# First tile of the input projection by row blocks of the weights, and output projection one product at a time

## The chip, the cores and the metric

The kernel runs on one core of one Trainium2 chip. The metric is the time of one execution on the device in microseconds; of several runs the median is compared. TensorE (PE) does matrix products and transposes into the eight banks of PSUM, the vector engine (DVE) and the scalar engine (ACT) do elementwise work, GpSimd (POOL) small elementwise work, and SyncE (SP) issues nearly all DMAs. Each engine runs its own instruction stream in order; they meet at semaphores.

## The reference

One layer of a hybrid decoder: 2048 tokens, width 1024, float32.

```
hn  = rmsnorm(x, g_mix_pre);  z = hn @ w_in            # 1024 -> 1604 columns
q, k, v, q_idx, k_idx, w_idx, zp = split(z)            # 8 query heads, 2 kv heads, 4 indexer heads
score[t,s] = sum_h w_idx[t,h] * relu(q_idx[t,h] . k_idx[s])    # causal
sel  = top-k keys of score per query, k = 256
attn = softmax over sel of (q . k) @ v                 # rotary on 16 dims of each head
pool = trailing means 2/4/8/16 of zp minus zp, a 128x128 map for each group, a scale
h  = x + rmsnorm(concat(attn, pool) @ w_o, g_mix_post)
h += rmsnorm(relu(rmsnorm(h, g_mlp_pre) @ w_up)^2 @ w_down, g_mlp_post)
h += rmsnorm(sigmoid(h @ w_ple_gate) * (p @ w_ple_proj), g_ple_post)
```

## The kernel before, in words

Tokens are cut into T = 16 tiles of 128, widths into K = 8 row blocks of 128. Where float32 accuracy matters an operand is split into a high part (type fp32r) and a low part, and a product is done as three matmuls, hi·hi, hi·lo and lo·hi (`split_product`).

**Stage 1, the input projection.** SP issues the small loads (pos_i, g_pre_col, pool_scale_col, g_mlp_col, w_pool_sb, all counted by `small_ld`), then x of tiles 0 and 1, then w_in in eight row blocks of 128 x 1604 (`w_in_raw`), counted by two semaphores of four blocks each. ACT makes `w_in_hi` (L930) with the gain g_pre, DVE `w_in_lo` (L1326). Ahead of that DVE computes the angles of the rotary tables (L1126 to L1140, each operation waiting for the one before) and ACT their sine (L854). For each tile ACT squares x (`square_x`), DVE and POOL make 1/rms and scale (`norm`), TensorE transposes x into banks 0 and 1 (`transpose_x`), ACT and DVE take it out in two halves as `hnT_hi` and `hnT_lo` (`evacuate_hnT`). TensorE then makes z of the tile in four column groups, `project_to` for banks 2 (0 to 512), 3 (to 1024), 4 (68 columns) and 5 (the pooling columns), each over k = 0 to 7. Between the groups of tile i stand `transpose_pool(i - 1)`, `transpose_k(i - 1)` and `transpose_x(i + 1)`. `rope` on DVE rotates q and k with the tables. The search for the top-k thresholds of tiles 2 to 7 runs on ACT and DVE beside the projection.

**Stage 2, the attention.** All (head, key block) pairs of all tiles are one list of steps m; a tile i has 8 heads of 1, 2, 3 or 4 key blocks (tiles 0 to 3, 4 to 7, 8 to 11, 12 to 15). At step m TensorE computes score blocks about two heads ahead (`score_block`, L1601 and L1602), transposes the probabilities of step m + 2 (`turn_probs`, L1687), multiplies those of step m with the values (`weigh`, L1701) and does index products of the search (`search_part`). DVE adds the mask and takes the maximum (`mask_block`, L1368), ACT does exp and copies the transposed probabilities to SBUF (`probsT`, L1015). The search of tiles 8 to 15 is spread over the steps up to head 5 of tile 13: each round has one count on DVE (L1230) and one on ACT (L912), and the threshold moves when both are done. Tile i - 1's output projection (16 products 128x128 by 128x512, L1721) is done in the heads of tile i: behind head 1 `transpose_o`; behind the last step of heads 2, 3 four products each into bank 0 for the left half of the columns (n = 0), behind heads 4, 5 for n = 1. ACT moves mixT out of PSUM at head 2 and the two results (`evacuate_mix`, L977 and L980) at heads 4 and 6.

```
if last_of(H, b) and i >= 1:
    if h == 1:
        transpose_o(i - 1)
    if h in (2, 3):
        output_projection(i - 1, 0, range(4 * (h - 2), 4 * (h - 1)))
    if h in (4, 5):
        output_projection(i - 1, 1, range(4 * (h - 4), 4 * (h - 3)))
```

**Stage 3, the MLP and the per-layer embedding**, in four chunks of 512 tokens, begins when stage 2 is over.

Of the kernel before, what the change touches and what calls it, by code (L numbers as in the profile page):

```python
# [47 lines left out]
def hybrid_block(nc, x, p, positions, g_mix_pre, w_in, w_pool, pool_scale, w_o, g_mix_post,  # L48
# [30 lines left out]
    with ExitStack() as ctx:  # L79
# [3 lines left out]
        def sem(name):  # L83
            return ctx.enter_context(nc.semaphore(name))
# [137 lines left out]
        w_in_ld = [sem("w_in_ld_low"), sem("w_in_ld_high")]  # L222
# [198 lines left out]

        AHEAD_BLOCKS = 2
# [100 lines left out]
        def over(cols, width):  # L523

            return cols.unsqueeze(2).to_broadcast([P, cols.shape[1], width])
# [10 lines left out]
        def _(sp):  # L536
            def row_over_partitions(dst, src):
                return sp.dma_start(dst, src.to_broadcast([P, D]))

            sp.dma_start(pos_i[:], positions[0].rearrange("(t p) -> p t", p=P),  # L540
                         allow_slow_non_contiguous=True).then_inc(small_ld, 16)
            for dst, src in ((g_pre_col, g_mix_pre), (pool_scale_col, pool_scale), (g_mlp_col, g_mlp_pre)):
# [4 lines left out]
            def load_x(i, u):  # L547
                sp.dma_start(x_in[:, u, :], x_tiles[i]).then_inc(x_ld[u], 16)

# [302 lines left out]
        def _(act):  # L852
            act.wait_ge(turns_rdy, 1)
            nc.scalar.activation(trig[:], turns[:], ACT.Sin).then_inc(trig_rdy, 1)  # L854

# [67 lines left out]
            act.wait_ge(setup_step, 4 + ROT_HALF + G)  # L923
            act.wait_ge(small_ld, 16 * 5)
            junk_early = kept_early[:, 512:1024].bitcast(BF16)
            square_x(0)
            square_x(1)
            for k in range(K):
                act.wait_ge(w_in_ld[k // (K // 2)], 16 * K // 2)
                nc.scalar.activation(w_in_hi[:, k, :], w_in_raw[:, k, :], ACT.Identity,  # L930
                                     scale=g_pre_col[:, k:k + 1]).then_inc(w_in_hi_rdy, 1)
# [3 lines left out]

            evacuate_hnT(0, 0)
            for i in range(T):
                evacuate_hnT(i, 1)
                if i >= 1:
                    copy_pool_rows(i - 1)  # L940
                if i + 2 < T:
                    square_x(i + 2)
                if i >= 1:
                    search_part(4 * i - 1, junk_early)
                evacuate_za(i, i % 2)
                if i >= 1:
                    evacuate_pool(i - 1)
                search_part(4 * i, junk_early)
                evacuate_zb(i, i % 2)
                if i >= 1:  # L950
                    evacuate_k(i - 1)
# [163 lines left out]
        def _(dve):  # L1115
            dve.wait_ge(small_ld, 16 * 5)
            dve.wait_ge(setup_step, 4 + ROT_HALF + G)
            done = [0]

            def link(ins):  # L1120
                done[0] += 1
                ins.then_inc(rot_setup, 1)
                dve.wait_ge(rot_setup, done[0])


            link(nc.vector.tensor_copy(pos_f[:], pos_i[:]))  # L1126
            link(nc.vector.tensor_tensor(angle[:], over(pos_f[:], ROT_HALF),
                                         freq[:].unsqueeze(1).to_broadcast([P, T, ROT_HALF]), ALU.mult))
            for n, (quarter, shift) in enumerate(((0.0, 0.0), (0.25, float(np.pi / 2)))):
                link(nc.vector.tensor_scalar(turns[:, n], angle[:], float(1 / (2 * np.pi)), quarter, ALU.mult, ALU.add))  # L1130
                link(nc.vector.tensor_scalar(turns[:, n], turns[:, n], ROUND, None, ALU.add))
                link(nc.vector.tensor_scalar(turns[:, n], turns[:, n], -ROUND, None, ALU.add))
                rest = angle[:]
                for part in TWO_PI:
                    link(nc.vector.scalar_tensor_tensor(out=trig[:, n], in0=turns[:, n], scalar=float(-part), in1=rest,
                                                        op0=ALU.mult, op1=ALU.add))
                    rest = trig[:, n]
                link(nc.vector.tensor_scalar(turns[:, n], trig[:, n], shift, None, ALU.add))
                link(nc.vector.tensor_scalar(turns[:, n], turns[:, n], PI_SAFE, -PI_SAFE, ALU.min, ALU.max))
            nc.vector.tensor_copy(rot[:, 0, 0:1, 0:1], turns[:, 0, 0:1, 0:1]).then_inc(turns_rdy, 1)  # L1140

# [23 lines left out]
            def rope(i, u):  # L1165
                dve.wait_ge(za_ev, i + 1)
# [153 lines left out]

            norm(0, 0)

            for k in range(K):

                dve.wait_ge(w_in_hi_rdy, k + 1)
                nc.vector.scalar_tensor_tensor(out=w_in_lo[:, k, :], in0=w_in_raw[:, k, :], scalar=g_pre_col[:, k:k + 1],  # L1326
                                               in1=w_in_hi[:, k, :].bitcast(F32), op0=ALU.mult,
                                               op1=ALU.subtract).then_inc(w_in_lo_rdy, 1)
            norm(1, 1)
            dve.wait_ge(trig_rdy, 1)  # L1330
            evacuate_hnT(0, 0)
            for i in range(T):
                evacuate_hnT(i, 1)
                if i >= 1:
                    rope(i - 1, (i - 1) % 2)
                    early_part(4 * i - 1)
# [5 lines left out]
                if i >= 1:  # L1342
                    evacuate_k(i - 1)
# [197 lines left out]
        def _(pe):  # L1541
            pe.wait_ge(const_rdy, sum(WINDOWS) - G + 2)
            pe.wait_ge(small_ld, 16 * 5)
# [25 lines left out]
            def pool_product(i):  # L1569
                pe.wait_ge(mixer_step, 10 * i + 9)  # L1570
# [11 lines left out]
            def project_to(b, lo, hi, done_sem, first=False, fresh=None, half_sem=None):  # L1582
                for k in range(K):
                    if fresh is not None and k % 4 == 0:
                        pe.wait_ge(hnT_lo_rdy, 2 * fresh + k // 4 + 1)
                    if first:
                        pe.wait_ge(w_in_lo_rdy, k + 1)
# [43 lines left out]

            transpose_x(0)
            for i in range(T):
                pe.wait_ge(za_ev, i)
                project_to(2, 0, Z_A, za_ps, i == 0, fresh=i)
                if i >= 2:
                    pool_product(i - 2)
                if i >= 1:
                    transpose_pool(i - 1)
# [3 lines left out]
                if i >= 1:  # L1643
                    transpose_k(i - 1, (i - 1) % 2)
# [100 lines left out]
            for m, (H, b) in enumerate(steps):  # L1745
# [131 lines left out]
```

## Time and profile before

| what | value |
|---|---|
| median of 3 runs | 3360.23 us (3358.62 to 3362.65) |
| the profiled execution | 3354.67 us |
| its span | 3353.1 us |
| its mean granted TensorE clock | 0.947 |
| TensorE, DVE, ACT, POOL busy | 3053.1, 1684.7, 1334.7, 336.3 us |
| stage 1, 2, 3 (from, to) | 0 to about 430, to about 1543, to 3353 us |

The profile is of one execution. A row of its timeline gives the start, the length and the engine of an instruction or of several merged ones; what stands in brackets is the idle time before it and what ended it. The clock column is the TensorE clock that was granted, as a share of 2.4 GHz. Matmul ends are modelled, so rows overlap a little. A few matmul records are missing.

### The profile page before, as it was taken

What the parts mean: (1) busy time and instruction counts of PE and PEld (TensorE: products, weight loads), DVE (VectorE), ACT (ScalarE), POOL (GpSimd) and SP (SyncE); (2) the same over time, 40 slices, a digit from 0 to 9 for tenths busy, and PEclk for the clock granted to TensorE, in tenths of its full rate; (3) what the DMA queues carried; (4) which work ended last, traced back from release to release, by engine and by line L of the source; (5) the groups of instructions that cost most, each with busy time, mean ns of one, the idle gap of its engine ahead of it and who ended that gap; (6) DMA issues with size and microseconds to landing.
All of it is one profiled execution on the core that took longest, in us unless ns stands there. A gap on an engine that the chain in (4) does not pass through costs nothing.

```text
span 3353.1 us, 38038 instructions
## 1 busy us (share of the span) xinstructions
PE 3053.1 (91%) x13944; PEld 2353.3 (70%) x13944; DVE 1684.7 (50%) x3373; ACT 1334.7 (40%) x2162; POOL 336.3 (10%) x431
## 2 busy tenths in 40 slices
PE   5999968788888888996999989999999999999998
PEld 4877856565666776884788847888568886588873
DVE  3376777777866777631333343333433333433333
ACT  3253455756656477553322223222232222222221
POOL 1332322121120310000000000000000000000000
PEclk9999989798887878998999999999999999999999
DMA  3111142111201110105423303233123322133210
GB/s 118 60 53 57 36 124 58 53 52 35 62 20 30 45 35 22 54 23 186 136 90 101 120 31 119 88 101 120 48 79 113 101 89 94 58 119 101 88 50 26
DMA packets 215456, 250.92 MB, mean 75 GB/s; under 512 B 57952, under 2 KB 160096, under 8 KB 215264
## 3 DMA queue, kind: packets, MB, share of 16 engines
q1 hardware_dynamic: 212960, 239.99, 22.5%
q10 hardware_dynamic: 2304, 8.39, 0.6%
q8 instruction: 118, 1.93, 0.2%
q14 instruction: 74, 0.61, 0.1%
HBM read 208.34 MB, written 40.01 MB: 74 GB/s over the span
## 4 chain that ended last, share of the span: by engine, by line
issue 59%; PE 26%; DVE 7%; ACT 4%; POOL 2%; DMA 1%; SPq 0%; DVEq 0%; POOLq 0%; ACTq 0%
PE bank L1579 7%; PE bank L1721 6%; PE bank L1701 5%; PE bank L1601 2%; PE bank L1687 2%; PE bank L1602 2%; ACT kept L912 2%; DVE kept L1230 1%; DVE probs L1368 1%; ACT probsT L1015 1%; ACT score_tail L912 1%; DVE too_few L1238 1%; POOL rstdC L847 1%; POOL score L823 1%; PE bank L1550 1%
## 5 line engine op out<-in xcount | busy, mean ns | idle before, releaser
L1443 DVE TENSOR_TENSOR w_lo<-w_raw,w_hi 128x1024 fp32r<-128x1024 f32 x256 | 312.6, 1222 | 520.5 <-ACT w_hi L1058 514.8
L1058 ACT CAST w_hi<-w_raw 128x1024 fp32r<-128x1024 f32 x256 | 267.4, 1045 | 562.0 <-PE bank L1579 535.0
L1701 PE MATMUL bank<-values,probsT 128*128 128x64 f32 x2176 | 334.7, 301 | 149.7 <-ACT probsT L1015 124.6
L1701 PEld LDWEIGHTS bank<-values,probsT 128*128 128x128 f32 x2176 | 313.7, 219 | 176.7 <-ACT probsT L1015 162.8
L1579 PE MATMUL bank<-hn_hi,w_hi 128*128 128x512 f32 x1024 | 400.3, 391 | 14.9 <-DVE hn_lo L1460 10.7
L1579 PE MATMUL bank<-w_hi,hid_lo 128*128 128x512 f32 x1024 | 405.9, 396 | 0.0
L1579 PE MATMUL bank<-w_lo,hid_hi 128*128 128x512 f32 x1024 | 405.9, 396 | 0.0
L1579 PE MATMUL bank<-w_hi,hid_hi 128*128 128x512 f32 x1024 | 405.9, 396 | 0.0
L1579 PE MATMUL bank<-hn_lo,w_hi 128*128 128x512 f32 x1024 | 399.7, 390 | 0.0
L1579 PE MATMUL bank<-hn_hi,w_lo 128*128 128x512 f32 x1024 | 399.4, 390 | 0.0
L1368 DVE CUSTOM_DVE_ANT_0 probs<-bank,mask 128x384 f32<-128x384 f32 (+3 forms) x320 | 193.7, 607 | 234.4 <-PE bank L1602 232.3
L912 ACT ACTIVATE kept<-score,threshold 128x1024 bf16<-128x1024 f32 (+4 forms) x160 | 251.9, 1574 | 112.2 <-DVE threshold L1247 91.8
L1230 DVE TENSOR_SCALAR_CACHE_REDUCE kept<-score,threshold 128x896 bf16<-128x896 f32 (+4 forms) x160 | 267.7, 1673 | 0.7
L1721 PE MATMUL bank<-wo_sb,mixT_t 128*128 128x512 f32 x512 | 247.0, 628 | 2.2 <-ACT h_t L980 1.1
L1478 DVE CAST hid_hi<-square 128x512 fp32r<-128x512 f32 x128 | 54.7, 427 | 366.0 <-ACT square L1083 366.0
L1081 ACT ACTIVATE square<-bank 128x512 f32<-128x512 f32 x128 | 76.6, 599 | 403.7 <-PE bank L1579 403.7
L1579 PEld LDWEIGHTS bank<-hn_hi,w_hi 128*128 128x128 f32 x1024 | 192.9, 188 | 56.9 <-issue 16.4
L1849 PE MATMUL bank<-w_gate_sb,h3T 128*128 128x512 f32 x512 | 227.1, 602 | 0.0
L1579 PEld LDWEIGHTS bank<-w_hi,hid_lo 128*128 128x128 f32 x1024 | 192.8, 188 | 47.0
L1579 PEld LDWEIGHTS bank<-w_hi,hid_hi 128*128 128x128 f32 x1024 | 192.9, 188 | 46.9
L1579 PEld LDWEIGHTS bank<-w_lo,hid_hi 128*128 128x128 f32 x1024 | 192.9, 188 | 46.9
L1579 PEld LDWEIGHTS bank<-hn_hi,w_lo 128*128 128x128 f32 x1024 | 192.9, 188 | 40.3
(191 smaller groups left out, 4754.4 us busy)
## 6 DMA issues: line engine op xcount, KB each, us to landing
w_raw<-in_w_up SPq DMA_DIRECT2D x64, 1024.0 KB, 5.6
w_raw<-in_w_down SPq DMA_DIRECT2D x64, 1024.0 KB, 5.0
x_in<-in_x SPq DMA_DIRECT2D x16, 512.0 KB, 3.7
q_t<-q_scratch SPq DMA_DIRECT2D x32, 256.0 KB, 3.7
x_t<-in_x SPq DMA_DIRECT2D x16, 512.0 KB, 4.3
h_scratch<-h_t SPq DMA_DIRECT2D x16, 512.0 KB, 2.9
hnT_scratch<-hn2T_t SPq DMA_DIRECT2D x16, 512.0 KB, 3.9
hn_lo<-hnT_scratch SPq DMA_DIRECT2D x4, 2048.0 KB, 11.3
```

The lines of the kernel that those rows point to most:

```text
L912: nc.scalar.activation(junk[:, 0:P * (t + 2)], score_of(t + 1), ACT.Sign, scale=-1.0, bias=threshold[:, 1:2].bitcast(F32), accum_out=below ...
L1058: nc.scalar.copy(w_hi[:, p % 4, :].rearrange("p (k f) -> p k f", f=piece_width(p)), raw_piece(p)).then_inc(w_hi_rdy, 1)
L1081: nc.scalar.activation(square[:, f % 2, :], bank[:, UP[q % 2][f % 2], :], ACT.Relu).then_inc(relu2_step, 1)
L1230: nc.vector.tensor_scalar(junk[:, 0:P * (t + 1)], score_of(t), threshold[:, 0:1].bitcast(F32), -float(P), ALU.is_lt, ALU.add, accum_out=be ...
L1368: nc.vector.tensor_tensor_reduce(out=probs[:, H % 3, o:o + w], in0=bank[:, ring_bank[("s", H, b)], 0:w], in1=mask[:, i % 2, o:o + w], scal ...
L1443: nc.vector.tensor_tensor(out_p, raw_piece(p), hi_p.bitcast(F32), ALU.subtract).then_inc(w_lo_rdy, 1)
L1579: ins = nc.tensor.matmul(dst, lhs[a], rhs[b], start=(first and n == 0), stop=(last and n == 2))
L1601: nc.tensor.matmul(dst, hi, k_parts[:, key, o:o + w], start=True, stop=False)
L1602: return nc.tensor.matmul(dst, lo, k_parts[:, key, o:o + w], start=False, stop=True)
L1701: last = nc.tensor.matmul(bank[:, 4, h * HEAD:(h + 1) * HEAD], probsT[:, m % 3, a * P:(a + 1) * P], values[:, kt, HEAD * kv:HEAD * (kv + 1 ...
L1721: last = nc.tensor.matmul(bank[:, mix_bank(i, n), :], mixT_t[:, k, :], wo_sb[:, k, n * 512:(n + 1) * 512], start=(k == 0), stop=(k == K - 1))
L1849: last = nc.tensor.matmul(bank[:, (2, 4)[n], :], h3T[:, a % 2, k, :], w_gate_sb[:, k, n * 512:(n + 1) * 512], start=(k == 0), stop=(k == K ...
```

## The change

The loads: x of tile 0 is issued first, then g_pre_col with a semaphore of its own, w_in row blocks 0 to 3, x of tile 1, blocks 4 to 7, and then the other small loads. Each row block has a semaphore. The first tile has a function of its own on TensorE, `project_first_tile`: k is the outer loop, and each k is multiplied into all four banks; `transpose_x(1)` stands after k = 5. ACT and DVE split the row blocks in three groups (0, 1 to 3, 4 to 7) with the hnT halves of tiles 0 and 1 and the squares and norms between them. The rotary tables are made behind the last hnT half of tile 1; ACT waits for them ahead of `copy_pool_rows(0)`, and `rope` waits for the sine. The loops over tiles start at 1.

In the attention the products of the output projection are laid out by a table `mix_at`: for each half n the eight k are spread over the steps of two heads after the first of them, and stand ahead of `weigh(m)`.

```diff
+        mix_at = {}
+        for i in range(1, T):
+            for n in range(2):
+                first = Q_HEADS * i + 2 + 2 * n
+                places = range(head_first[first] + 1, head_first[first + 2])
+                for k in range(K):
+                    mix_at.setdefault(places[k * len(places) // K], []).append((i - 1, n, k))
...
+            load_x(0, 0)
+            sp.dma_start(g_pre_col[:], g_mix_pre[0].rearrange("(k p) -> p k", p=P),
+                         allow_slow_non_contiguous=True).then_inc(g_pre_ld, 16)
+            load_w_in(range(0, K // 2))
+            load_x(1, 1)
+            load_w_in(range(K // 2, K))
             sp.dma_start(pos_i[:], positions[0].rearrange("(t p) -> p t", p=P),
...
-            load_x(0, 0)
-            load_x(1, 1)
-            for k in range(K):
-                sp.dma_start(w_in_raw[:, k, :], w_in[0, k * P:(k + 1) * P, :]).then_inc(w_in_ld[k // (K // 2)], 16)
...
+            square_x(0)
+            act.wait_ge(g_pre_ld, 16)
+            split_weights(range(0, 1))
             evacuate_hnT(0, 0)
+            evacuate_hnT(0, 1)
+            split_weights(range(1, 4))
+            square_x(1)
+            split_weights(range(4, K))
+            evacuate_hnT(1, 0)
+            evacuate_za(0, 0)
+            evacuate_hnT(1, 1)
+            evacuate_zb(0, 0)
+            evacuate_zc(0, 0)
+            act.wait_ge(setup_step, 4 + ROT_HALF + G)
+            act.wait_ge(small_ld, 16 * 4)
+            act.wait_ge(turns_rdy, 1)
+            nc.scalar.activation(trig[:], turns[:], ACT.Sin).then_inc(trig_rdy, 1)
+            copy_pool_rows(0)
+            square_x(2)
...
             norm(0, 0)
+            dve.wait_ge(g_pre_ld, 16)
+            split_weights(range(0, 1))
+            evacuate_hnT(0, 0)
+            evacuate_hnT(0, 1)
+            split_weights(range(1, 4))
+            norm(1, 1)
+            split_weights(range(4, K))
+            evacuate_hnT(1, 0)
+            evacuate_hnT(1, 1)
+            rotations()
+            norm(2, 0)
...
+            def project_first_tile():
+
+                for k in range(K):
+                    if k % 4 == 0:
+                        pe.wait_ge(hnT_lo_rdy, k // 4 + 1)
+                    pe.wait_ge(w_in_lo_rdy, k + 1)
+                    for b, lo, hi, done_sem in ((2, 0, Z_A, za_ps), (3, Z_A, Z_B, zb_ps), (4, Z_B, Z_POOL, zc_ps), (5, Z_POOL, W_IN, zp_ps)):
+                        last = split_product(bank[:, b, 0:hi - lo], (hnT_hi[:, k, :], hnT_lo[:, k, :]),
+                                             (w_in_hi[:, k, lo:hi], w_in_lo[:, k, lo:hi]), k == 0, k == K - 1)
+                        if k == K - 1:
+                            last.then_inc(done_sem, 1)
+                    if k == 3:
+                        last.then_inc(half_used, 1)
+                    if k == 5:
+                        transpose_x(1)
...
+                for i_mix, n, k in mix_at.get(m, ()):
+                    output_projection(i_mix, n, range(k, k + 1))
                 weigh(m)
...
-                    if h in (2, 3):
-                        output_projection(i - 1, 0, range(4 * (h - 2), 4 * (h - 1)))
-                    if h in (4, 5):
-                        output_projection(i - 1, 1, range(4 * (h - 4), 4 * (h - 3)))
```

## Rows read from the trace of the kernel before

**Rows 1.** The page: busy us, share of the span, instructions.

```profile
PE 3053.1 (91%) x13944; PEld 2353.3 (70%) x13944; DVE 1684.7 (50%) x3373; ACT 1334.7 (40%) x2162; POOL 336.3 (10%) x431
```

**Rows 2.** Timeline of the start: start us, us, engine line op out<-in.

```profile
0.73 0.43 SPq L540 DMA_DIRECT2D pos_i<-in_positions  x1
...
6.96 0.17 DVE L1126 CAST pos_f<-pos_i 128x16 f32<-128x16 int32 x1 [6.96 <-DMA w_pool_sb<-in_w_pool]
...
12.57 1.04 ACT L900 ACTIVATE score_tail<-x_in 128x1024 bf16<-128x1024 f32 x1
...
15.54 1.94 PE L1550 MATMUL bank<-ident,x_in 128*128 128x128 f32 x8 [15.54 <-DVE x_in L1146]
...
18.12 6.20 ACT L930 ACTIVATE w_in_hi<-w_in_raw,g_pre_col 128x1604 fp32r<-128x1604 f32 x4 [3.19 <-DMA w_in_raw<-in_w_in]
...
27.94 7.29 DVE L1326 SCALAR_TENSOR_TENSOR w_in_lo<-w_in_raw,g_pre_col,w_in_hi 128x1604 fp32r<-128x1604 f32 x4 [0.86 <-ACT w_in_hi L930]
...
36.63 1.28 DVE L1151 TENSOR_TENSOR hnT_lo<-bank,hnT_hi 128x512 fp32r<-128x512 f32 x2
...
37.41 0.77 PE L1579 MATMUL bank<-w_in_hi,hnT_hi 128*128 128x512 f32 x1 [19.93 <-DVE hnT_lo L1151]
```

**Rows 3.** Tile w_in_raw and tile x_in: loads of each, and time to landing.

```profile
L557 SPq DMA_DIRECT2D w_in_raw<-in_w_in x8: 432/448/652, 5.4 to 9.2; - x8
...
DMA to landing us min/median/max: 6.8/12.1/17.0
...
DMA to landing us min/median/max: 3.4/4.7/10.0
```

**Rows 4.** The timeline of the scalar engine at the first change of tile.

```profile
60.38 0.59 ACT L885 CAST hnT_hi<-bank 128x512 fp32r<-128x512 f32 x1 [2.17 <-PE bank L1579]
...
65.86 0.60 ACT L860 ACTIVATE zs<-bank 128x512 f32<-128x512 f32 x1 [3.36 <-PE bank L1579]
```

**Rows 5.** The timeline of the scalar engine at its first table load.

```profile
0.74 1.28 ACT L854 ACT_TABLE_LOAD   x1 [0.74 <-PEq L1866]
```

**Rows 6.** The waits of 586 to 1360 us: total us, times, longest.

```profile
DVE probs L1368 <- PE bank L1602: 130.2, 65, 6.9
...
PE bank L1701 <- ACT probsT L1015: 107.8, 69, 4.6
```

**Rows 7.** The timeline of TensorE and of the vector engine around one projection run.

```profile
976.43 6.17 PE L1721 MATMUL bank<-wo_sb,mixT_t 128*128 128x512 f32 x8
...
983.10 0.69 DVE L1368 CUSTOM_DVE_ANT_0 probs<-bank,mask 128x512 f32<-128x512 f32 x1 [6.00 <-PE bank L1602]
```

**Rows 8.** Windows: length, busy PE, PEld, DVE, ACT, POOL, clock, DMA.

```profile
964.00:967.00 3.00, 3.00 (x7) 1.30 (x7) 0.22 (x2) 1.00 (x2) 0.00 (x0) 0.93 0.00 0
...
973.00:976.00 3.00, 1.70 (x10) 1.46 (x9) 2.93 (x8) 2.54 (x4) 0.00 (x0) 0.78 0.00 0
...
976.00:979.00 3.00, 3.00 (x6) 1.55 (x7) 1.10 (x2) 2.68 (x5) 0.00 (x0) 0.50 0.00 0
```

**Rows 9.** Windows over heads 2 to 5 of eight of the tiles.

```profile
549.00:580.00 31.00, 29.54 (x137) 19.18 (x135) 20.72 (x37) 10.38 (x22) 12.72 (x14) 1.00 0.20 51
...
608.00:641.00 33.00, 28.35 (x119) 18.56 (x118) 19.51 (x62) 20.60 (x41) 0.00 (x0) 0.87 0.08 17
...
664.00:697.00 33.00, 28.48 (x134) 19.28 (x134) 23.61 (x73) 24.20 (x43) 0.00 (x0) 0.95 0.07 17
...
794.00:835.00 41.00, 33.99 (x156) 23.55 (x157) 25.71 (x70) 27.24 (x43) 0.00 (x0) 0.88 0.06 14
...
943.00:994.00 51.00, 43.58 (x199) 30.40 (x197) 30.86 (x76) 28.16 (x42) 7.92 (x8) 0.87 0.05 11
...
1035.00:1089.00 54.00, 45.16 (x204) 31.79 (x203) 33.12 (x84) 35.28 (x51) 0.00 (x0) 0.83 0.05 10
...
1230.00:1289.00 59.00, 49.29 (x232) 37.47 (x232) 39.59 (x95) 40.64 (x56) 0.00 (x0) 0.82 0.04 9
...
1404.00:1446.00 42.00, 42.00 (x261) 32.75 (x260) 12.61 (x38) 19.07 (x32) 0.00 (x0) 1.00 0.00 1
```

More of the change, by code:

```diff
@@ L219, in hybrid_block @@
         mlp_stack.close()
-        w_in_ld = [sem("w_in_ld_low"), sem("w_in_ld_high")]
+        g_pre_ld = sem("g_pre_ld")
+        w_in_ld = [sem(f"w_in_ld_{k}") for k in range(K)]
         w_in_hi_rdy = sem("w_in_hi_rdy")
@@ L921, in search_part, with split_weights @@
                     count_below(t, k, junk)
-            act.wait_ge(setup_step, 4 + ROT_HALF + G)
-            act.wait_ge(small_ld, 16 * 5)
-            junk_early = kept_early[:, 512:1024].bitcast(BF16)
[L926 to L931, printed above, removed]
+            def split_weights(ks):
+                for k in ks:
+                    act.wait_ge(w_in_ld[k], 16)
+                    nc.scalar.activation(w_in_hi[:, k, :], w_in_raw[:, k, :], ACT.Identity,
+                                         scale=g_pre_col[:, k:k + 1]).then_inc(w_in_hi_rdy, 1)
+            junk_early = kept_early[:, 512:1024].bitcast(BF16)
             def copy_pool_rows(i):
@@ L934, in copy_pool_rows @@
                 nc.scalar.copy(zp_rows[:], bank[:, 5, :]).then_inc(zp_rows_ev, 1)
+            square_x(0)
+            act.wait_ge(g_pre_ld, 16)
+            split_weights(range(0, 1))
             evacuate_hnT(0, 0)
-            for i in range(T):
-                evacuate_hnT(i, 1)
-                if i >= 1:
+            evacuate_hnT(0, 1)
[13 more added lines that the diff above has]
+            square_x(2)
+            for i in range(1, T):
+                if i >= 2:
+                    evacuate_hnT(i, 1)
                     copy_pool_rows(i - 1)
@@ L1115, in _ @@
         def _(dve):
[L1116 to L1140, printed above, removed]
             def norm(i, u):
@@ L1165, in rope @@
             def rope(i, u):
+                dve.wait_ge(trig_rdy, 1)
                 dve.wait_ge(za_ev, i + 1)
@@ L1319, in early_part @@
                 weigh_early(at["index"].get(spot, ()))
-            norm(0, 0)
[L1323 to L1328, printed above, removed]
-            norm(1, 1)
-            dve.wait_ge(trig_rdy, 1)
@@ L1331, in _, with rotations, link @@
[L1331 to L1336, printed above, removed]
+            def rotations():
+                dve.wait_ge(small_ld, 16 * 4)
+                dve.wait_ge(setup_step, 4 + ROT_HALF + G)
+                done = [0]
+                def link(ins):
+                    done[0] += 1
+                    ins.then_inc(rot_setup, 1)
+                    dve.wait_ge(rot_setup, done[0])
+                link(nc.vector.tensor_copy(pos_f[:], pos_i[:]))
+                link(nc.vector.tensor_tensor(angle[:], over(pos_f[:], ROT_HALF),
+                                             freq[:].unsqueeze(1).to_broadcast([P, T, ROT_HALF]), ALU.mult))
+                for n, (quarter, shift) in enumerate(((0.0, 0.0), (0.25, float(np.pi / 2)))):
+                    link(nc.vector.tensor_scalar(turns[:, n], angle[:], float(1 / (2 * np.pi)), quarter, ALU.mult, ALU.add))
+                    link(nc.vector.tensor_scalar(turns[:, n], turns[:, n], ROUND, None, ALU.add))
+                    link(nc.vector.tensor_scalar(turns[:, n], turns[:, n], -ROUND, None, ALU.add))
+                    rest = angle[:]
+                    for part in TWO_PI:
+                        link(nc.vector.scalar_tensor_tensor(out=trig[:, n], in0=turns[:, n], scalar=float(-part), in1=rest,
+                                                            op0=ALU.mult, op1=ALU.add))
+                        rest = trig[:, n]
+                    link(nc.vector.tensor_scalar(turns[:, n], trig[:, n], shift, None, ALU.add))
+                    link(nc.vector.tensor_scalar(turns[:, n], turns[:, n], PI_SAFE, -PI_SAFE, ALU.min, ALU.max))
+                nc.vector.tensor_copy(rot[:, 0, 0:1, 0:1], turns[:, 0, 0:1, 0:1]).then_inc(turns_rdy, 1)
@@ new lines, in split_weights @@
+            def split_weights(ks):
+                for k in ks:
+                    dve.wait_ge(w_in_hi_rdy, k + 1)
+                    nc.vector.scalar_tensor_tensor(out=w_in_lo[:, k, :], in0=w_in_raw[:, k, :], scalar=g_pre_col[:, k:k + 1],
+                                                   in1=w_in_hi[:, k, :].bitcast(F32), op0=ALU.mult,
+                                                   op1=ALU.subtract).then_inc(w_in_lo_rdy, 1)
+            norm(0, 0)
+            dve.wait_ge(g_pre_ld, 16)
@@ new lines, in _ @@
+            split_weights(range(0, 1))
+            evacuate_hnT(0, 0)
+            evacuate_hnT(0, 1)
+            split_weights(range(1, 4))
+            norm(1, 1)
+            split_weights(range(4, K))
[3 more added lines that the diff above has]
+            norm(2, 0)
+            for i in range(1, T):
+                if i >= 2:
+                    evacuate_hnT(i, 1)
+                rope(i - 1, (i - 1) % 2)
+                early_part(4 * i - 1)
@@ L1630, in search_part @@
                 index(at["index"].get(spot, ()))
+            def project_first_tile():
[12 more added lines that the diff above has]
+                        transpose_x(1)
             transpose_x(0)
-            for i in range(T):
+            project_first_tile()
+            for i in range(1, T):
                 pe.wait_ge(za_ev, i)
-                project_to(2, 0, Z_A, za_ps, i == 0, fresh=i)
+                project_to(2, 0, Z_A, za_ps, fresh=i)
                 if i >= 2:
                     pool_product(i - 2)
-                if i >= 1:
-                    transpose_pool(i - 1)
+                transpose_pool(i - 1)
                 search_part(4 * i)
@@ L1642, in _ @@
                 project_to(3, Z_A, Z_B, zb_ps)
-                if i >= 1:
-                    transpose_k(i - 1, (i - 1) % 2)
+                transpose_k(i - 1, (i - 1) % 2)
                 search_part(4 * i + 1)
```

34 lines of the change are left out of this document (15 added, 19 removed).

## The prediction

> **What bounds the kernel now.** I read the page first. TensorE is busy 91% of the span, so the question is where the other 9% lies and at which clock the 91% is spent [rows 1]. The 40 slices show three stages: the projection of x to about 430 us, the attention with its top-k search to about 1543 us, the MLP from there. The change touches the start of the first and heads 2 to 5 of each tile of the second. The MLP has no edited line and no start time of its own, so it moves as a block.
>
> *The start.* The timeline shows the vector engine making the rotation tables first, from 6.96 us; the sine must be done before the scalar engine squares x (12.57), so tile 0 is transposed only at 15.54 [rows 2]. The weights land one row block per 2.0 us: eight loads issued from 5.4 to 9.2 us take 6.8 us (the first) to 17.0 us (the last), so blocks 0 to 7 arrive at 12.2, 14.2 ... 26.2 [rows 3]. Two semaphores, each for four blocks, let the split into high and low parts begin only at 18.12 and 26.27; the last low part ends at 27.94 + 7.29 = 35.2, and TensorE's first projection matmul starts at 37.41 [rows 2]. From there TensorE sets the pace: tile 0 ends at 60.4, where the scalar engine can take the next hnT half, and the first column group of tile 1 at 65.9 [rows 4].
>
> *The attention.* By the waits of 586 to 1360 us TensorE waits 107.8 us in L1701 for the scalar engine's copy of probsT, and the vector engine waits 130.2 us for score blocks [rows 6]. Both hang together around the output projection. One product of it is two recorded passes; a run of four lasts about 3.65 us at full clock, longer at half. In the timeline the run that begins at 976.43 keeps the score matmuls away until 982; the vector engine idles 6.00 us up to 983.10, so the counting of the search stops too [rows 7]. In the steps ahead of such a run it is TensorE that idles: 1.70 us busy of 3 just before the run, after which the granted clock is 0.50, that is 1.2 GHz instead of 2.4, and it is at this clock that the run starts [rows 8].
>
> **Part 1, the first tile.** Removed from the path: the rotation chain, the sine and four small loads ahead of x; the two four-block waits; and the order by column group (bank 2, then 3, 4, 5). Nothing is added: 96 projection matmuls as before, k outermost. Worked forward:
> - x is issued at 0.73. A load of its size took 3.4 us alone [rows 3], so it lands at 4.2. From the square over the norm to the first transpose takes 15.5 − 12.6 = 3.0 us, the transposes 1.94 [rows 2]: done at 9.1.
> - g_pre_col and block 0 are issued behind x. x and block 0 together are 1.3 MB; I put block 0 at 6.9, the next at 2.0 us each, and x of tile 1 (1.3 us) in fourth place: 8.9, 10.9, 12.9, then 16.1 to 22.1.
> - High parts cost 1.55 us each, low parts 7.29/4 = 1.82, an hnT half 0.65 [rows 2]. Low part 0 ends at 10.4, the two hnT halves at 11.1 and 11.7. The first projection matmul starts at **11.1**. Low parts 1 to 3 end at 13.6 to 17.2, the norm of tile 1 at 18.8, low parts 4 to 7 at 20.6 to 26.1.
> - TensorE needs 60.38 − 37.41 = 22.97 us for the tile, cold start and the transposes of tile 1 included [rows 2, 4], about 2.4 us per k at full clock (a 512-wide column group takes 5.5 us for its 24 matmuls [rows 4], 0.23 each; a k has nine of these and three narrow ones) and 4 in the first. It never overtakes the low parts (k = 7 begins near 31.5 and needs 26.1), so the tile ends at 11.1 + 23.0 = **34.1**, against 60.4: 26.3 us earlier.
> - The new wait. On the scalar engine the sine stands ahead of copy_pool_rows(0), and TensorE's transpose_pool(0) stands ahead of the second column group of tile 1. The vector engine comes free after its last hnT half (about 35.4) and needs 12.6 − 7.0 = at most 5.6, nearer 5.3, for the rotations: 40.7. Sine 0.4 and copy 0.6: 41.7. TensorE arrives after the first column group of tile 1, at 34.1 + 5.5 = 39.6 [rows 4], and waits **2.1 us**. Behind it the square and norm of tile 2 (3.0, as in tile 0) and rope of tile 0 follow by about 46; transpose_k(0) and the transposes of tile 2 come at 47 and later, so nothing more is late.
> - A second table load. The first load stands at 0.74 in front of the sine [rows 5]. If Square as first function draws another set, the sine needs 1.28 more, between 0 (hidden in the wait for the rotations) and 1.3. I take 0.6.
> - The small loads now queue behind the weights, on SP and in the DMA engines. They land by about 25 and are wanted at 35 at the earliest: nothing. SP's next wait is for the transposes of x, as before.
>
> Part 1 gains 26.3 − 2.1 − 0.6 = **24 us**; bounds 20 (blocks 2 us late, 3.3 of wait) and 26.
>
> The Trainium skill ("ScalarE: Activation LUTs", What ACT_TABLE_LOAD costs) gives a switch of set a drain of 1.38 us beside the load; the trace has the 1.28 of the load [rows 5], and by the page the term would be up to 2.7 instead of 0.6. Nothing else here uses it.
>
> **Part 2, the output projection.** The same 16 products per tile. For n = 0 they now lie over the steps of heads 2 and 3 after the first, for n = 1 over heads 4 and 5, each between turn_probs(m + 2) and weigh(m), where TensorE waits for probsT. With one block per head (tiles 1 to 3) there is one place, so eight products in one run; with two blocks (4 to 7) 3, 3, 2; with three (8 to 11) 2, 2, 1, 2, 1; with four (12 to 15) 2 and then one each. New waits: the first product of a half waits for mixT_rdy or mix_ev. The scalar engine does either ahead of the probsT copy that weigh(m) of the same step waits for anyway, so they cost nothing.
>
> What can be won in a tile is the way from its present window (rows 9 are of tiles 3, 4, 5, 7, 9, 10, 12 and 14) to the larger of two works: vector busy, and TensorE busy at full clock. A share (1 − clock) of the window is what the lower clock added.
> - Tiles 9, 10, 12: windows 51, 54, 59; TensorE 43.6 − 0.13·51 = 37, 45.2 − 9.2 = 36, 49.3 − 10.6 = 39, vector 31, 33, 39.6 [rows 9]. Room 14 + 18 + 19 = 51.
> - Tiles 4, 5, 7: windows 33, 33, 41; TensorE 24, 27, 29; room 9 + 6 + 12 = 27.
> - Tiles 6, 11, 13, 14, 15: TensorE never idle at full clock, like the row of 1404 to 1446, where the vector engine is only 12.6 us busy. Room 0; the order of products on the bound engine is no gain. Tile 8 has 3.
> - Tiles 1 to 3: TensorE busy 29.5 of 31 [rows 9]; two runs of 7.3 us in place of four of 3.65. Loss between 0 and 3.65 × 6 = 22; it is the bound engine, so I take 3.
>
> I take half of the 51 (in tile 9 the vector engine needs 31/12 = 2.6 us for a step; TensorE has 37 us with 16 products of 0.9, so 1.9 of its own per step and 0.9 for a product, which nearly fits, but some places have two), a quarter of the 27, and 1 for tile 8: 25 + 7 + 1 − 3 = **30 us**. Bounds −22 and +81.
>
> **The sum.** 3354.7 − 24 − 30 = 3300.7 for the profiled execution. The median, 3360.2, is 5.6 above it, so I predict **3306** (−1.6%).
>
> **Rivals.**
> - *A: the products are no cheaper spread* (they push score blocks back by the same sum, or the idle time only moves to other steps). For: the vector engine's idle time beside the runs is only part of its 130 us. Against: rows 7. Time 3360 − 24 = 3336. Chance 0.27.
> - *B: the room is nearly all taken*, with a steady clock: 3360 − 24 − 65 = 3271. For: the room in rows 9. Against: two or three products in most places. Chance 0.12.
> - *C, the slower one: the clock.* The runs of four are what lifts the granted clock back to 1.00 after each idle stretch (in 964 to 967 it is at 0.93 again [rows 8]). Without them tiles 1 to 12 could stay low for longer. If the mean clock over 500 to 1360 fell by 0.08, 0.08 × 860 = 69 us are lost: 3360 − 24 + 69 = 3405; it decides from a fall of 0.03 (24 us). Against: spread products fill the very stretches that sink it. The Trainium skill ("TensorE: Matmul & The Clock Gate", A second HAM failure mode) describes a kernel whose short idle times between matmul groups made the clock oscillate, which speaks for C; no row here shows a spread projection. Chance 0.06.
> - *D: part 1 is eaten* by weights that land late or by a wait I missed in tile 1, part 2 stays small: 3355. Chance 0.05.
>
> **Chances and range.** Both parts pay, 3282 to 3326: 0.50. A 0.27, B 0.12, C 0.06, D 0.05. The range takes in A: 3280 to 3340. 0.2% is 6.7 us, about what a measurement can tell from no change. Faster: all but C and half of D, 0.92; same 0.03; slower 0.05.
>
> **What would show it.** In the changed profile the first projection matmul at 11 us, tile 0 over at 34, tile 1 some 24 us before its present end; a wait of about 2 us before the transposes of zp_rows; no wait for w_in_lo. Then: L1701's wait for probsT falls, tiles 9, 10 and 12 shorten by 7 to 10 us each and their clock rises, tiles 11 and 13 to 15 keep their length, the MLP too. I am wrong if TensorE waits for low parts in the first tile, if the clock of tiles 4 to 12 falls, or if runs of eight cost tiles 1 to 3 more than some us.

## The result, and the profile after

The changed kernel takes 3281.4 us (median of 4 runs, 3279.3 to 3281.9), the kernel before 3359.4 us in the same comparison: 78 us less, a ratio of 0.977 with a 95% interval of 0.976 to 0.978. Forecast were 3306 us and a gain of 54. The time lies in the range stated, 1.4 us above its low end, and just under the case with the highest chance (3282 to 3326).

The page of the changed kernel, against [rows 1]:

```profile
span 3277.7 us, 38057 instructions
...
PE 3025.7 (92%) x13944; PEld 2335.0 (71%) x13944; DVE 1684.6 (51%) x3373; ACT 1335.1 (41%) x2163; POOL 336.6 (10%) x431
...
PEclk9999979798889989998999999999999999999999
```

TensorE is busy 27 us less for the same 13944 matmuls, and the rest of the span is 252 us instead of 300. So of the 75 us that the span lost, 48 are TensorE's idle time, and 27 are time that the same matmuls no longer take: the mark of a higher clock. The same line of the page of the kernel before has lower digits in the slices of the attention:

```profile
PEclk9999989798887878998999999999999999999999
```

The split is not sharp. In a second profile of the changed kernel (span 3280.1 us) TensorE is busy 3035.2 us, so that there 18 of 73 us are busy time and 55 idle time.

The timeline of the start and of one step in tile 9, against [rows 2, 4, 5, 7]:

```profile
4.67 1.06 ACT L911 ACTIVATE score_tail<-x_in 128x1024 bf16<-128x1024 f32 x1 [2.65 <-DMA x_in<-in_x]
...
6.92 15.83 SPq L569 DMA_DIRECT2D pool_scale_col<-in_pool_scale  x1
...
7.94 1.63 ACT L937 ACTIVATE w_in_hi<-w_in_raw,g_pre_col 128x1604 fp32r<-128x1604 f32 x1 [2.12 <-DMA w_in_raw<-in_w_in]
...
12.23 0.80 PE L1613 MATMUL bank<-w_in_hi,hnT_hi 128*128 128x512 f32 x1 [2.64 <-DVE hnT_lo L1149]
...
23.33 1.64 ACT L937 ACTIVATE w_in_hi<-w_in_raw,g_pre_col 128x1604 fp32r<-128x1604 f32 x1 [0.70 <-DMA w_in_raw<-in_w_in]
...
34.15 0.59 ACT L896 CAST hnT_hi<-bank 128x512 fp32r<-128x512 f32 x1 [1.16 <-PE bank L1613]
...
40.74 1.28 ACT L961 ACT_TABLE_LOAD   x1 [5.04 <-DVE rot L1345]
...
42.98 1.12 PE L1582 MATMUL bank<-ident,zp_rows 128*128 128x128 f32 x4 [3.35 <-ACT zp_rows L943]
...
60.03 0.59 ACT L896 CAST hnT_hi<-bank 128x512 fp32r<-128x512 f32 x1 [2.18 <-PE bank L1613]
...
928.60 0.49 PE L1734 MATMUL bank<-ident,probs 128*128 128x128 f32 x3
...
928.92 1.02 PE L1768 MATMUL bank<-wo_sb,mixT_t 128*128 128x512 f32 x2
...
929.78 1.00 PE L1748 MATMUL bank<-values,probsT 128*128 128x64 f32 x8
```

x is squared at 4.67, and the first projection matmul runs at 12.23 instead of 37.41. Tile 0 is over at 34.15 (the second hnT half of tile 1), as against 60.38. Then the sine's table load starts only when the rotations are done (40.74), TensorE waits 3.35 us for the pooling rows, and tile 1 is over at 60.03. The same row of the kernel before stands at 81.32, so tile 1 is over 21.3 us earlier:

```profile
81.32 0.59 ACT L885 CAST hnT_hi<-bank 128x512 fp32r<-128x512 f32 x1 [2.21 <-PE bank L1579]
```

By the first transposes of o_sb, in tile 1 of the attention, 18.1 us of it are left (452.5 instead of 470.6). This stage varies by some us from one profile to the next: with the old start and the new attention (an experiment below) the same transposes stand at 474.0. The last three rows are one product (two passes) between the transposes of step m + 2 and weigh: no idle time stands ahead of L1748.

The windows of the stretch behind that wait and of heads 2 to 5 of tiles 4, 5, 7, 9, 10, 12 and 14 (columns as in [rows 8]), against [rows 9]:

```profile
43.00:46.00 3.00, 3.00 (x9) 2.54 (x10) 1.33 (x5) 2.92 (x6) 0.55 (x1) 0.51 0.00 0
...
592.00:617.00 25.00, 25.00 (x114) 17.20 (x113) 18.84 (x61) 19.55 (x39) 0.00 (x0) 0.93 0.10 23
...
640.00:667.00 27.00, 26.93 (x128) 18.68 (x128) 21.48 (x68) 22.05 (x41) 0.00 (x0) 0.94 0.09 20
...
767.00:798.00 31.00, 30.08 (x152) 21.13 (x153) 24.47 (x67) 26.31 (x41) 0.00 (x0) 0.96 0.08 18
...
908.00:947.00 39.00, 36.59 (x194) 25.51 (x194) 29.89 (x76) 26.42 (x41) 8.53 (x8) 1.00 0.06 14
...
987.00:1026.00 39.00, 36.65 (x201) 26.01 (x201) 33.32 (x84) 34.22 (x50) 0.00 (x0) 0.99 0.06 14
...
1166.00:1212.00 46.00, 43.98 (x229) 32.87 (x228) 37.06 (x92) 37.24 (x52) 0.00 (x0) 0.89 0.05 12
...
1329.00:1371.00 42.00, 42.00 (x258) 32.50 (x257) 12.70 (x38) 19.53 (x33) 0.00 (x0) 1.00 0.00 1
```

The first row is at 0.51: behind the wait the clock was 1.2 GHz for most of 3 us. The windows of tiles 4, 5, 7, 9, 10, 12 shrank from 33, 33, 41, 51, 54 and 59 us to 25, 27, 31, 39, 39 and 46, and TensorE is idle in them for 2.4 us at most. The clock rose in all of them but tile 5 (0.95 to 0.94). Tile 14 kept its 42.

The waits of the same tiles, against [rows 6]:

```profile
PE bank L1748 <- ACT probsT L1039: 80.8, 51, 4.7
...
DVE probs L1401 <- PE bank L1634: 40.9, 50, 2.4
```

TensorE waits 81 us instead of 108 for probsT, the vector engine 41 instead of 130 for score blocks. A part of this has moved: for the index products of the search (tiles `weighed` and `score`) the vector engine waited 21 us before and waits 48 now:

```profile
DVE weighed L1216 <- PE bank L1634: 31.4, 21, 3.2
...
DVE score L1216 <- PE bank L1634: 16.1, 7, 4.3
```

### The profile page after: what moved, and what is told of

Its sections match the earlier page's. It is cut to its first block, busy times and chain, and to the rows that moved or that the text cites. A ratio compares the mean times of both kernels' runs of the same rounds, so it can differ in the third digit from the quotient of the medians.

```text
span 3277.7 us, 38057 instructions
## 1 busy us (share of the span) xinstructions
PE 3025.7 (92%) x13944; PEld 2335.0 (71%) x13944; DVE 1684.6 (51%) x3373; ACT 1335.1 (41%) x2163; POOL 336.6 (10%) x431
## 4 chain that ended last, share of the span: by engine, by line
issue 62%; PE 24%; DVE 7%; ACT 4%; POOL 2%; DVEq 0%; POOLq 0%; ACTq 0%
PE bank L1613 7%; PE bank L1748 5%; PE bank L1768 4%; PE bank L1633 2%; PE bank L1734 2%; PE bank L1634 2%; ACT kept L923 1%; DVE kept L1229 1%; DVE probs L1401 1%; POOL score L837 1%; POOL rstdC L861 1%; PE bank L1582 1%; ACT probsT L1039 1%; ACT probs L1026 1%; DVE too_few L1237 0%
## 5 line engine op out<-in xcount | busy, mean ns | idle before, releaser
L1748 PEld LDWEIGHTS bank<-values,probsT 128*128 128x128 f32 x2176 | 314.3, 214 | 206.4 <-ACT probsT L1039 141.6
L1748 PE MATMUL bank<-values,probsT 128*128 128x64 f32 x2176 | 323.8, 294 | 123.0 <-ACT probsT L1039 97.0
```

The lines of the kernel that those rows point to most:

```text
L1748: last = nc.tensor.matmul(bank[:, 4, h * HEAD:(h + 1) * HEAD], probsT[:, m % 3, a * P:(a + 1) * P], values[:, kt, HEAD * kv:HEAD * (kv + 1 ...
```

## The experiments

All times are medians, each with the kernel before on the same chip (3357.6 to 3358.8 there). In the table the last columns are read from each timeline: the distance between the transposes of o_sb in tile 1 and in tile 4, and between those in tile 4 and in tile 13, in the profiled execution. They hold the products that are done in the heads of tiles 1 to 3 and of tiles 4 to 12.

| kernel | start | output projection | us | ratio to before (95%) | tiles 1-3 | tiles 4-12 |
|---|---|---|---|---|---|---|
| before | old | runs of 4, behind weigh | 3359.4 | | 137.1 | 729.4 |
| changed | new | spread, ahead of weigh | 3281.4 | 0.977 (0.976 to 0.978) | 139.1 | 670.3 |
| start alone | new | runs of 4, behind | 3337.5 | 0.9935 (0.991 to 0.996) | 138.1 | 733.3 |
| projection alone | old | spread, ahead | 3301.2 | 0.983 (0.981 to 0.985) | 138.9 | 672.5 |
| spread behind | new | spread, behind | 3331.4 | 0.992 (0.991 to 0.994) | 159.7 | 699.1 |
| runs of four ahead | new | runs of 4, ahead | 3308.0 | 0.986 (0.984 to 0.988) | 140.5 | 689.8 |
| runs of eight | new | runs of 8, ahead | 3347.9 | 0.997 (0.996 to 0.998) | 139.1 | 727.7 |
| transposes twice | new | runs of 4, behind | 3325.6 | 0.990 (0.989 to 0.992) | 138.7 | 715.6 |

**The start alone.** The lines of the projection go back, and the table `mix_at` goes:

```diff
-                for i_mix, n, k in mix_at.get(m, ()):
-                    output_projection(i_mix, n, range(k, k + 1))
                 weigh(m)
...
+                    if h in (2, 3):
+                        output_projection(i - 1, 0, range(4 * (h - 2), 4 * (h - 1)))
+                    if h in (4, 5):
+                        output_projection(i - 1, 1, range(4 * (h - 4), 4 * (h - 3)))
```

> Only the new start of the projection; the output projection in runs of four as before. Theory (the two parts add): tile 1 ends 21.3 us earlier as in the changed kernel, the attention is that of the kernel before, so the time is 18 to 22 us under the kernel before (about 3339). Rival (the parts interact, the gain in the attention comes with the earlier start or with the clock's phase): more than 30 us or less than 10 us under it.

Measured: 21.3 us under the kernel before; the interval is wide, 14 to 30 us, so that the 21.3 of the timeline of the changed kernel is the firmer number. The attention is about as long as before (tiles 4 to 12 733 instead of 729 us).

**The projection alone.** The start goes back to the old one, `mix_at` stays.

> Only the products of the output projection spread over the steps; the start as before. Theory: 52 to 60 us under the kernel before (about 3303), all of it in the attention, with tiles 9, 10 and 12 shorter by 13, 17 and 11 us. Rival as in the run with the start alone: below 45 us or above 70 us.

Measured: 57.6 us under the kernel before. 21.3 + 57.6 = 79 against 78 for both: the parts add, and the second is worth nearly three times the first. Tiles 9, 10 and 12 are shorter by 12, 16 and 9 us, where 13, 17 and 11 were expected.

**Spread, but behind weigh; and runs of four, but ahead of it.** Two things changed at once in the second part, the length of a run and its place. Each is tried without the other:

```diff
-                for i_mix, n, k in mix_at.get(m, ()):
-                    output_projection(i_mix, n, range(k, k + 1))
                 weigh(m)
+                for i_mix, n, k in mix_at.get(m, ()):
+                    output_projection(i_mix, n, range(k, k + 1))
```

> The changed kernel, but each product stands behind weigh(m) instead of ahead of it. Theory L (what pays is that the runs are short, so that score blocks never wait long): at most 8 us above the changed kernel (3281 to 3289). Theory P (what pays is the place ahead of weigh, in TensorE's wait for probsT): most of the 57 us is lost, 3320 to 3340.

```diff
-                places = range(head_first[first] + 1, head_first[first + 2])
                 for k in range(K):
-                    mix_at.setdefault(places[k * len(places) // K], []).append((i - 1, n, k))
+                    mix_at.setdefault(head_first[first + 1 + k // 4] - 1, []).append((i - 1, n, k))
```

> The changed kernel, but the products in runs of four at the last step of heads 2, 3, 4, 5 as before, moved ahead of weigh(m). Theory L (short runs): 3325 to 3345, near the kernel with the new start alone. Theory P (the place): 3281 to 3300.

Measured: 3331.4 and 3308.0. Theory L, with which I went in, is wrong for the first: spreading alone is worth only 6 us of the 56 between the start alone and the changed kernel. Theory P is too simple for the second, which lies between the two forecasts: the place alone is worth 30. In tiles 4 to 12 each alone gives 34 to 44 us and both together 63; what undoes "spread behind" are tiles 1 to 3, where a head has one block and the eight products are one run: 160 us instead of 139. TensorE's timeline in tile 2 of that kernel shows how:

```profile
506.35 0.91 PE L1748 MATMUL bank<-values,probsT 128*128 128x64 f32 x6 [3.42 <-ACT probsT L1039]
...
507.06 8.78 PE L1768 MATMUL bank<-wo_sb,mixT_t 128*128 128x512 f32 x16
...
515.28 0.79 PE L1633 MATMUL bank<-k_parts,q_hi 128*128 128x512 f32 x1
```

First TensorE waits 3.42 us for probsT, then weighs, then multiplies for 8.8 us, and the next score block comes at 515.28. The wait and the run stand one after the other, and the run begins at half clock: at full clock it lasts 7.03 us. In the changed kernel the same run lies over the wait, and the next score block is late by the longer of the two, not by their sum:

```profile
495.23 7.03 PE L1768 MATMUL bank<-wo_sb,mixT_t 128*128 128x512 f32 x16
502.10 0.78 PE L1748 MATMUL bank<-values,probsT 128*128 128x64 f32 x6
502.68 0.47 PE L1633 MATMUL bank<-k_parts,q_hi 128*128 128x512 f32 x1
```

**Runs of eight.** All products of a half at the last step of head 3 or head 5, ahead of weigh:

```diff
-                    mix_at.setdefault(places[k * len(places) // K], []).append((i - 1, n, k))
+                    mix_at.setdefault(places[-1], []).append((i - 1, n, k))
```

> The changed kernel, with all eight products of a half in one run at the last step of head 3 and of head 5, ahead of weigh. Both the length of a run and the place have turned out to count. If length costs what it cost between one or two products and runs of four (tiles 4 to 12 became 20 us longer), eight give another 20 to 40 us: 3325 to 3350. Rival (only the place counts, and a run as a whole pays its stall once, so half as many runs cost no more): 3300 to 3312, like runs of four ahead of weigh.

Measured: 3347.9, 66 us above the changed kernel, within what was expected of a cost by length. In tiles 4 to 12 the distance is 670 spread, 690 in runs of four, 728 in runs of eight, and there the vector engine waits 41, 63 and 99 us for score blocks, at most 2.4, 4.0 and 7.5 us at a time. Another 8 us are lost in tile 13, outside the columns of the table. These numbers fit the reading that a wait hides no more of a run than its own length; no run measures that length by itself.

**Every transpose twice.** This tells whether the clock is a part of the gain. In the kernel with the new start alone, TensorE repeats the transposes of the probabilities in heads 2 to 5 of six tiles. Both times the same values go to the same place:

```diff
-                for a in range(w // P):
+                twice_over = H // Q_HEADS in (4, 5, 7, 9, 10, 12) and H % Q_HEADS in (2, 3, 4, 5)
+                for a in list(range(w // P)) * (2 if twice_over else 1):
                     last = nc.tensor.transpose(bank[:, 1 + m % 3, a * P:(a + 1) * P],
```

> The kernel with the new start alone (products in runs of four behind weigh), but in heads 2 to 5 of tiles 4, 5, 7, 9, 10 and 12 every transpose of the probabilities is done twice, ahead of weigh: about 29 us more work for TensorE, put where it waits for probsT. Theory K (half of the gain is the clock, which the filled waits keep up): the added work costs nothing or less than nothing; the time is between 15 us below and 5 us above the kernel with the new start alone (3338) and the clock of these tiles rises. Theory F (only the filled wait itself counts): TensorE's filled waits give nothing back, the time rises by 5 to 25 us.

Measured: 3325.6, 12 us *under* the start alone, with 212 matmul records more. The intervals of the two ratios overlap slightly, but all four runs (3322.5 to 3326.7) lie under all four of the start alone (3331.0 to 3344.1). Theory F, a rise of 5 to 25 us, is out. Windows of heads 2 to 5 of tiles 9, 10 and 12, first with the start alone:

```profile
931.00:984.00 53.00, 46.20 (x197) 32.10 (x196) 30.89 (x76) 28.17 (x42) 7.94 (x8) 0.81 0.05 11
...
1023.00:1077.00 54.00, 45.28 (x206) 32.95 (x206) 33.00 (x84) 35.57 (x52) 0.00 (x0) 0.84 0.05 10
...
1215.00:1278.00 63.00, 53.07 (x239) 39.75 (x239) 39.81 (x96) 41.17 (x56) 0.00 (x0) 0.78 0.04 9
```

and with the transposes done twice:

```profile
929.00:978.00 49.00, 43.94 (x234) 32.72 (x233) 30.88 (x76) 28.16 (x42) 7.98 (x8) 0.93 0.05 12
...
1016.00:1068.00 52.00, 43.76 (x236) 32.73 (x235) 33.19 (x84) 35.43 (x51) 0.00 (x0) 0.93 0.05 11
...
1204.00:1260.00 56.00, 46.70 (x281) 36.70 (x281) 41.28 (x101) 40.78 (x55) 0.00 (x0) 0.97 0.05 10
```

The clock rises from 0.81, 0.84, 0.78 to 0.93, 0.93, 0.97, and TensorE is busy 134.4 us instead of 144.6 although it does more. The vector engine's work is the same within 2 us, so the windows are not shorter for less work; what has changed in TensorE's favour is the clock. In tiles 4 to 12 a pass of the output projection takes 617 ns in the mean instead of 665 (592 is its time at full clock), and TensorE's total busy time there is 598 us instead of 609.

**The sine behind the pooling rows.**

```diff
-            act.wait_ge(setup_step, 4 + ROT_HALF + G)
-            act.wait_ge(small_ld, 16 * 4)
-            act.wait_ge(turns_rdy, 1)
-            nc.scalar.activation(trig[:], turns[:], ACT.Sin).then_inc(trig_rdy, 1)
             copy_pool_rows(0)
             square_x(2)
+            act.wait_ge(setup_step, 4 + ROT_HALF + G)
+            act.wait_ge(small_ld, 16 * 4)
+            act.wait_ge(turns_rdy, 1)
+            nc.scalar.activation(trig[:], turns[:], ACT.Sin).then_inc(trig_rdy, 1)
```

> The changed kernel, with the copy of the pooling rows and the square of tile 2 on the scalar engine ahead of the sine and its table load. Theory (the wait of 3.35 us and the half clock behind it cost about 5 us): TensorE no longer waits ahead of the transposes of zp_rows, tile 1 ends 4 to 5 us earlier, and the time is 3 to 6 us under the changed kernel (3281). Rival (the wait only moves, to the k transposes, which wait for rope and so for the sine): no more than 1 us earlier at the end of tile 1.

Measured: 3278.1 (ratio 0.976, 0.975 to 0.978), 3 us under the changed kernel, which the intervals alone would not tell apart. The scalar engine's timeline does:

```profile
41.30 1.28 ACT L963 ACT_TABLE_LOAD   x1 [3.52 <-DVE rot L1345]
...
46.18 0.37 ACT L877 COPY zs<-bank 128x256 f32<-128x256 f32 x1 [1.17 <-PE bank L1613]
```

The table load now runs while TensorE multiplies; the second column group of tile 1 is ready at 46.18 instead of 50.59, and no wait for zp_rows is left; the granted clock is 1.00 from 39 to 48 us. Tile 1 ends 4.4 us earlier than in the changed kernel (55.63). The rival is out.

**The first tile by column groups**, k inside, with the new loads:

```diff
-                for k in range(K):
...
-                    for b, lo, hi, done_sem in ((2, 0, Z_A, za_ps), (3, Z_A, Z_B, zb_ps), (4, Z_B, Z_POOL, zc_ps), (5, Z_POOL, W_IN, zp_ps)):
+                for b, lo, hi, done_sem in ((2, 0, Z_A, za_ps), (3, Z_A, Z_B, zb_ps), (4, Z_B, Z_POOL, zc_ps), (5, Z_POOL, W_IN, zp_ps)):
+                    if b == 5:
+                        transpose_x(1)
+                    for k in range(K):
...
```

> The changed kernel, but the first tile is projected column group by column group, k inside. Theory: the first group then ends no earlier than the last low part (27), and three groups and the transposes of tile 1 (15 us) come behind it, so tile 0 ends at 42 to 43 instead of 34.2 and the time is 7 to 9 us above the changed kernel. Rival (the early loads and waits alone give the gain): at most 2 us above.

Measured: 3290.2, 9 us above the changed kernel. Its waits on TensorE up to 65 us (total us, times, longest) have one that the changed kernel has not:

```profile
PE bank L1613 <- DVE w_in_lo L1350: 3.4, 6, 1.7
```

Only 3.4 us, but the first group is drawn out to the pace of the low parts while three quarters of the work wait behind it; tile 0 ends at 45.1 instead of 34.15, two to three us later than expected. The profiled execution is the slowest of its four, so the 9 us of the medians is the number for the whole kernel.

**The weights awaited by halves.**

```diff
-                    act.wait_ge(w_in_ld[k], 16)
+                    act.wait_ge(w_in_ld[K // 2 * (k // (K // 2)) + K // 2 - 1], 16)
```

> The changed kernel, but the split of the weights waits for four row blocks at a time, as before. Theory: the first high part starts at about 13.5 instead of 7.9, the first projection matmul at about 18 instead of 12.2, and TensorE stays the bound from there, so tile 0 and all behind it are 5 to 7 us later. Rival (TensorE waits for the low parts of the second half as well): 9 us or more.

Measured: 3284.3, 3 us above the changed kernel by the medians and 5.3 by the spans of the profiled executions. The first projection matmul comes at 18.30 instead of 12.23:

```profile
PE bank L1613 <- DVE hnT_lo L1149: 8.7, 1, 8.7
```

Tile 0 ends 7.0 us later (41.11), and at the first transposes of o_sb 5.1 us of it are left. The intervals of the medians alone would not tell the two kernels apart; the timeline does.

**The changed kernel again.**

> The changed kernel as it is, on the chip of the other two, to compare with them and to see how its half-clock stretches repeat: 3279 to 3284; the 3.4 us wait for the pooling rows in tile 1 and the stretch at half clock behind it are there again, while the steps of 1.5 to 3 us late in the projection stage come and go.

Measured: 3281.1. Tile 0 ends 1.1 us later than in the first profile, the wait of 3.3 us is there again, and the clock of the 3 us behind it is 0.56.

**A better version: the index products ahead of weigh, too**, on top of the sine behind the pooling rows:

```diff
+                search_part(EARLY_SPOTS + m)
                 weigh(m)
                 if m == Y_STEP:
                     pool_product(T - 1)
-                search_part(EARLY_SPOTS + m)
```

> The kernel with the sine behind the pooling rows, and the index products of the search, too, ahead of weigh(m) instead of behind it. Theory P (work ahead of weigh fills TensorE's wait for probsT): tiles that index in the late search (4, 6, 8, 9, 11 and 12 or so) have most of the remaining wait; 5 to 25 us below the kernel with the sine moved (3278). Rival (index products wait for the banks of the ring, and weigh now stands behind that wait): equal or up to 20 us slower.

Measured: 3262.9, a ratio of 0.972 (0.970 to 0.973) to the kernel before, 15 us under the kernel with the sine moved alone and 18 under the changed one. Its profiled execution is the slowest of its four (3258 to 3273), and in it tiles 4 to 12 take 664 us; which tiles give the rest I can't say from it.

## Why the prediction was right, and where its sizes were off

**Part 1: 24 us forecast, 21.3 measured.** The step "first projection matmul at 11.1" came at 12.23: block 0 landed about a microsecond later than I had put it, as did the later ones (the last high part starts at 23.33). The step "22.97 us for the tile" was too long by as much (21.92): TensorE left half clock 3.1 us after its first projection matmul, not 5.3 us as in the kernel before. Tile 0 ended at 34.15 against 34.1. That the two errors cancel is luck. TensorE never waited for a low part. The term "new wait, 2.1 us, and 0.6 for a table load" was too small: the load starts only at 40.74, when the rotations are done, so it counts in full, and the wait is 3.35 us. What the sum lacked is the clock behind the wait: 0.51 over 3 us, 1.5 us. 26.2 − 3.35 − 1.5 = 21.3. The sine experiment gets 4.4 of these 4.9 back. Of the gain, the k-outer loop is worth 9 us and the waits for single blocks 3 to 5; no run takes the new order of the loads or the later rotations by itself. By the Trainium skill ("ScalarE: Activation LUTs", What ACT_TABLE_LOAD costs) the change of set would cost 2.7 us; here the load took 1.28, began 0.1 us after the rotations and the sine followed at once, so that the trace shows no drain on the path; the scalar engine had been idle for 5.04 us before.

**Part 2: 30 us forecast, 57.6 measured.** The frame held: tiles 11, 13, 14 and 15 did not change, tiles 1 to 3 lost 2 us (3 forecast), and the gain came in tiles 4, 5, 7, 9, 10 and 12, bounded by the larger of vector work and TensorE work at full clock. The step that failed is the share: "half of the 51, a quarter of the 27". In rows of windows, tiles 9, 10 and 12 gave 12 + 15 + 13 = 40 of 51, tiles 4, 5 and 7 gave 8 + 6 + 10 = 24 of 27; the other heads of tiles 4, 5 and 7 gave 6 of it back. (Tile 8, for which no row stood behind the 3 us of room, gave 0.9.) The reason given for the half was that the places with two products would not fit a step. The timeline of tile 9 has such a place, four passes, and TensorE still waits behind it:

```profile
925.23 1.88 PE L1768 MATMUL bank<-wo_sb,mixT_t 128*128 128x512 f32 x4
...
927.47 0.88 PE L1748 MATMUL bank<-values,probsT 128*128 128x64 f32 x6 [0.35 <-ACT probsT L1039]
```

The experiments show what else the share left out. The place ahead of weigh lays a run over a wait, so a run of three or four costs only what the wait does not cover (30 us by itself). And the two losses seem to feed each other: behind sparse steps the run begins at half clock [rows 8], and a slow run keeps the score blocks away for longer. The doubled transposes show that filling the wait raises the clock; that this is why most of the room went at once is my reading.

The range held by 1.4 us only, and through its width: part 2 gave nearly twice what was forecast. Rival B (nearly all the room, 3271, chance 0.12) was nearer to the result than the forecast: of the 78 us of room in the six windows 64 went.

**Rival C, the clock: it mattered, but the other way.** The clock of tiles 4 to 12 did not fall (0.85 before, 0.88 after); products laid into the waits keep it up, as even useless transposes do. The Trainium skill ("TensorE: Matmul & The Clock Gate", A second HAM failure mode) names short idle times between groups as what lets the clock go; that agrees with the experiment that filled them, 0.81 to 0.93 in tile 9. The rival, that the runs of four lift the clock, left out that they begin at the low level, which the prediction had read in [rows 8] itself.

**Rival A** (spread products are no cheaper) would have been nearly true, had the products stood behind weigh: 6 us. The reason would not have been A's: in the profiles 34 us were gained in tiles 4 to 12 and 22 lost in tiles 1 to 3.

Not settled: how the gain of the second part divides between clock and waits. By the page of before and after, 27 of 75 us are busy time and 48 idle time, of which the start has some 22; by the second profile of the changed kernel 18 and 55. The two may cause one another, and no experiment held the clock still.

## What to carry to other kernels

Where an in-order engine has a wait of some length at a fixed point of a loop, try loose work directly ahead of that wait, in pieces no longer than it; behind the wait the same pieces added to it here (50 us of 3281). Then look who waits for the pieces of work that now come later, as for the index products here. Before pricing TensorE work that is moved, look at the granted clock at which it runs now: here a run behind a sparse stretch began at 0.50, and work that filled such stretches was cheaper than free. When a new wait enters TensorE's path, add what the clock loses behind it (1.5 us behind 3.35 here).

## What the runs showed of the hardware that I had not expected

- Adding 212 matmul records made the kernel 12 us faster, and TensorE's busy time in three windows fell from 144.6 to 134.4 us.
- A wait of 3.35 us in an otherwise dense stretch cost another 1.5 us at half clock.
- SyncE's issue of a small load behind the weights (pool_scale_col at 6.92) took 15.8 us, where the same issue took 0.6 us in front of them. It ended at 22.75, shortly before the last row block was there (23.33), and the profiles of the other kernels with the new start show 15.4 to 16.1 us for it. That SyncE was held by the weights ahead on its queue is my reading; no run moves this load alone. So x of tile 2 was asked for only at 24 us. It cost nothing here: x of tile 2 was wanted at 42.8 and the small loads at 35; in this place a load that is wanted before 24 us would have come late.
